# Moving the gate's four chunks and its split inside an output block, one chunk of the next layer's modulation, and one convolution tap, in a two-layer hybrid decoder kernel

## What is computed

```
mod = silu(c) @ w_ada + b_ada;  shift, scale, gate = split(mod, 3)
h   = rmsnorm(x, norm_pre) * (1 + scale) + shift
z   = h @ w_in                      # 2048 x 14336: gb, gcin, u, g_c, q, k, v, g_r
y_conv = gb * causal_conv3(gcin * u) * silu(g_c)
y_ret  = groupnorm(retention(rope(q), rope(k), v)) * silu(g_r)
o   = concat(y_conv, y_ret) @ w_out # 4096 x 2048
x   = x + gate * rmsnorm(o, norm_post)
```

## Time and profile before

| | us |
|---|---|
| median of three runs | 1730.23 |
| the profiled execution, whole | 1728.81 |
| its span, first to last instruction | 1727.0 |
| TensorE busy with matmuls | 1685.4 (98%) |
| VectorE busy | 1161.1 (67%) |
| ScalarE busy | 719.5 (42%) |

### The profile page before, as it was taken

One profiled execution on the slowest core, in us unless ns is written; L12 is line 12 of the kernel. 1 busy time (PEld: TensorE's weight loads), 2 busy tenths in 40 slices (PEclk: granted clock), 3 DMA queues, 4 the chain that ended last, 5 costly groups with the idle time before them and its releaser, 6 DMA issues. The chain is left out here.

```text
span 1727.0 us, 18943 instructions
## 1 busy us (share of the span) xinstructions
PE 1685.4 (98%) x7707; PEld 1376.3 (80%) x7707; DVE 1161.1 (67%) x1296; ACT 719.5 (42%) x802; POOL 51.0 (3%) x94
## 2 busy tenths in 40 slices
PE   6999999999999999999999999999999999999997
PEld 3567878888888888778878888888888888888886
DVE  2788767788578868777776456556555654567776
ACT  3344444434444444343455444444434444444332
POOL 4000000000000000000000000000000000000000
PEclk9999999999999999999999999999999999999999
DMA  9998655787788769877775666567556756668774
GB/s 341 383 383 316 211 180 191 271 293 263 253 289 312 270 217 323 321 274 284 282 248 164 197 203 196 189 196 219 193 178 202 216 187 189 209 242 303 290 286 179
DMA packets 233655, 429.25 MB, mean 249 GB/s; under 512 B 8664, under 2 KB 50024, under 8 KB 232800
## 3 DMA queue, kind: packets, MB, share of 16 engines
q1 hardware_dynamic: 225888, 408.97, 68.5%
q10 hardware_dynamic: 7680, 19.07, 4.0%
HBM read 417.57 MB, written 2.10 MB: 243 GB/s over the span
## 5 line engine op out<-in xcount | busy, mean ns | idle before, releaser
L809 DVE TENSOR_TENSOR w_lo<-stage,w_hi 128x1024 fp32r<-128x1024 f32 x574 | 692.9, 1223 | 467.2 <-ACT w_hi L588 464.5
L588 ACT CAST w_hi<-stage 128x1024 fp32r<-128x1024 f32 x574 | 595.7, 1051 | 945.6 <-PE Z L1275 576.2
L1273 PE MATMUL Z<-w_hi,H 128*128 128x512 f32 x1784 | 702.6, 394 | 11.0 <-DVE w_lo L809 6.4
L1275 PE MATMUL Z<-w_hi,H 128*128 128x512 f32 x1784 | 695.6, 390 | 0.0
L1274 PE MATMUL Z<-w_lo,H 128*128 128x512 f32 x1784 | 695.1, 390 | 0.0
L1273 PEld LDWEIGHTS Z<-w_hi,H 128*128 128x128 f32 x1784 | 335.3, 188 | 88.9 <-issue 8.0
L1275 PEld LDWEIGHTS Z<-w_hi,H 128*128 128x128 f32 x1784 | 335.3, 188 | 70.7
L1274 PEld LDWEIGHTS Z<-w_lo,H 128*128 128x128 f32 x1784 | 335.5, 188 | 67.9
L830 DVE SCALAR_TENSOR_TENSOR acc<-stage,c_silu,acc 128x512 f32<-128x512 f32 x240 | 180.2, 751 | 6.8
L1273 PE MATMUL Z<-w_hi,YR 128*128 128x512 f32 x256 | 100.2, 391 | 2.8 <-DVE w_lo L809 2.8
L1273 PE MATMUL Z<-w_hi,YC 128*128 128x512 f32 x256 | 99.7, 389 | 0.0
(11 more groups left out here) (160 smaller groups left out, 735.0 us busy)
## 6 DMA issues: line engine op xcount, KB each, us to landing
stage<-in_w_in SPq DMA_DIRECT2D x186, 1024.0 KB, 5.2
stage<-in_w_ada SPq DMA_DIRECT2D x64, 1024.0 KB, 7.4
stage<-in_w_out SPq DMA_DIRECT2D x64, 1024.0 KB, 7.4
stage<-in_w_in SPq DMA_DIRECT2D x74, 512.0 KB, 5.6
front_stage<-in_w_ada SPq DMA_DIRECT2D x32, 1024.0 KB, 11.2
behind<-R ACTq DMA_DIRECT2D x14, 448.0 KB, 3.5
taps<-in_conv_w ACTq DMA_DIRECT2D x18, 256.0 KB, 6.5
xt<-in_x SPq DMA_DIRECT2D x2, 1024.0 KB, 6.7
```

The source lines that it names most:

```text
L588: N.copy(w_bufs(n, h)[0], stage[:, slot_of(n), 2 * h:2 * h + 2, :]).then_inc(s_hi, 1)
L809: V.tensor_tensor(lo, stage[:, slot_of(n), 2 * h:2 * h + 2, :], hi.bitcast(F32), ALU.subtract)\
L1273: T.matmul(z[:, i, :], hh, wh, start=ch.first and a == 0, stop=False)
L1275: ins = T.matmul(z[:, i, :], hl, wh, start=False, stop=stop)
```

## The change

- The gate's chunks move from places 0, 2, 4, 5 of an output block to places 0, 2, 3, 4; in the very first output block (layer 0, block 0) they stand at 1, 2, 3, 4.
- `gate_parts` moves on VectorE from behind place 6 to behind place 5. TensorE's two matmuls stay at place 6 and `gate_row` stays at place 7.
- The first chunk of the first modulation sum of layer 1 moves from step 10 to step 11 of turn 1.
- The first tap of the first turn moves from step 9 to step 11.

The load order follows from `load_table`. In seven of the eight output blocks it becomes g0 w0 w1 g1 w2 g2 w3 g3 w4 w5 w6 w7, and in the first one w0 g0 w1 g1 w2 g2 w3 g3 w4 w5 w6 w7.

```diff
@@ FIRST
-                 tr=17, yrhi=19, yrlo=20, gcopy=99, cu=8, back=9, tap=(9, 14, 15), sg=9, gate=10,
+                 tr=17, yrhi=19, yrlo=20, gcopy=99, cu=8, back=9, tap=(11, 14, 15), sg=9, gate=10,
@@ ADA_CHUNKS
-    (1, (10, 12, 15, 16)), (1, (20, 23, 26, 27)), (2, (3, 4, 7, 8)), (2, (12, 15, 16, 18)),
+    (1, (11, 12, 15, 16)), (1, (20, 23, 26, 27)), (2, (3, 4, 7, 8)), (2, (12, 15, 16, 18)),
...
-GATE_CHUNKS, GATE_SUM, GATE_AT = (0, 2, 4, 5), 6, 7
+GATE_PARTS, GATE_SUM, GATE_AT = 5, 6, 7
+
+def gate_chunks(l, j):
+    return (0, 2, 3, 4) if l + j else (1, 2, 3, 4)
@@ load_table
-        if c.out and c.g in GATE_CHUNKS:
-            table.append(("gate", NB * c.l + c.j, GATE_CHUNKS.index(c.g)))
+        if c.out and c.g in gate_chunks(c.l, c.j):
+            table.append(("gate", NB * c.l + c.j, gate_chunks(c.l, c.j).index(c.g)))
@@ VectorE
-                if ch.out and ch.g in GATE_CHUNKS:
-                    kc = GATE_CHUNKS.index(ch.g)
+                if ch.out and ch.g in gate_chunks(ch.l, ch.j):
+                    kc = gate_chunks(ch.l, ch.j).index(ch.g)
                     ada_chunk(("gate", NB * ch.l + ch.j, kc), kc, ada_seen)
                     ada_seen += 1
...
-                if ch.out and ch.g == GATE_SUM:
+                if ch.out and ch.g == GATE_PARTS:
                     gate_parts(ch.l, ch.j)
```

## The result

The changed kernel takes 1737.27 us, the median of six runs (1735.58 to 1739.19), against 1730.08 us (1729.31 to 1731.41). The ratio is 1.0042 with a 95% interval of 1.0029 to 1.0055: slower by 7.2 us, where +4.7 was forecast.

The account below looks back on a forecast made before the run. TensorE, busy 1685.4 of 1727.0 us, was taken as the bound, so only its waits mattered. Terms 8.4 + 0.6 + 1.5 - 2.5 - 3.3 = +4.7 us gave a median of 1734.9 us, 8-in-10 range 1729 to 1740.

Parts of the forecast that it names:

- The tap: First turn's first tap, moved to step 11: the 2.51 us wait at 244.1 us goes, a gain of 2.5 us.
- The modulation chunk: Turn 1 of layer 1's first modulation sum: low parts are over 5 us early there, so priced at 0.
- The gate's split: Last block of each layer: waits of 1.88 and 1.43 us ahead of the gate's matmuls go, a gain of 3.3 us.
- The six later blocks: Blocks 1 to 3 of each layer: w4 comes late and TensorE stalls 1.4 us in each, a loss of 8.4 us.
- The deciding step: Blocks 1 to 3 of each layer: g1's slot goes to g3, so w4 lands 2.66 us later, slack 1.40 becoming -1.26 us.
- Layer 1's first block: Its w4 takes g3's place, landing after 8.9 us beside ScalarE's rows, slightly late: a loss of 0.6 us.
- The very first block: Layer 0, block 0: w3, held up by ScalarE's rows, stalls TensorE 3.5 us; present stalls go; a loss of 1.5 us.
- The signs in the profile: One w4 wait of 1.3 to 1.5 us per later block, none at gate's matmuls or 244 us, 3.5 to 4 at first-block w3.
- The faster rival: Six later blocks: w4 lands within 6.1 us of its issue, no stall, 1722 to 1725 us; chance 0.14.

Follow-up runs that it names:

- the fastest kernel: The changed kernel with w4 loaded ahead of g3 and the gate's rows fetched in quarters, those of blocks 1 to 3 one block ahead: 1719.83 us, ratio 0.9934.

## Why the prediction was right, and where it was not

**The tap** was priced at 2.5 us; 2.33 in the profile, 3.3 by the run of the tap alone, whose interval holds 2.5.

**The modulation chunk**, priced at 0, is 0.

**The gate's split**, priced at 3.3 us, brought 2.6 alone. What I said of its cause was incomplete: the new load order removes the same two waits without it, in part by making TensorE late.

**The six later blocks.** The deciding step was right: the slot of g1 goes to g3, w4 queues behind it, lands about 2.6 us later (0.41 + 7.3 - 5.1), and its slack of 1.40 us becomes a wait. Five of the six waits are 1.08 to 1.37 us. A listed wait begins at the end of the matmul before, 0.16 us behind the next start that would have been due (0.39 - 0.23), so the five starts came 1.24 to 1.53 us late, against 1.4 priced; exchanging the two loads removes them all. The term was mis-sized, 12.0 against 8.4, for three reasons.
First, the claim that the second of the pair took 7.4 to 7.5 us "in all six blocks" was wrong for block 1 of layer 0. Line 547, issued at 771.6 us in the kernel before, took this:

```profile
DMA to landing us min/median/max: 8.7/8.7/8.7
```

The changed kernel's w4 took 8.9 us in its place and waited 2.74 us, not 1.4. The other kernels show 8.5 to 8.9 us there too, so it belongs to that stretch. The DMA queues of the changed kernel from 772 to 779.7 us, while this load is under way, hold a line that they don't hold beside w4 in the next block (819.3 to 826.7 us), which took 7.3 us:

```profile
q8 instruction: 1, 0.02, 0.9%
```

This is one packet of 16 KB of instructions. 0.9% of 16 engines over 7.7 us is 1.1 us on one engine, near to the 1.3 to 1.5 us by which the load is late. In all fourteen profiles such a packet runs beside this load. In those of the kernel before and the changed one none runs beside the same loads of the other five blocks. No run moved it, so this cause isn't tested. A part of the error is the prediction's own besides: it priced all six blocks with a slack of 1.40 us, though it had read 0.96 us in this one.
Second, behind that wait the clock fell. The drop and the restart made another 1.4 us (4.26 lost, 2.90 of them up to w4's start). The prediction had no term for the clock and read it as full "in all slices of the page". A slice of the page is 43 us long and its digit 9 means 90% or more, so it hides the drop that a window from 92 to 96 us shows in the profile before (a mean granted clock of 0.57).
Third, each of the five other waits cost 0.15 us more than the late start, because the first matmuls behind it start further apart (0.33 us, then 0.23).

**Layer 1's first block** was priced at 0.6 and cost 2.0. I had put w3 in the place of g2, landing after 9.8 us. It stood behind g2 and took 11.4 us beside the rows; g3 and w4 then queued behind it, and w4 took 9.8 us where I had 8.9. The step that went wrong is the single price of 8.9 us, taken from a queue with less ahead of it.

**The very first block** was priced at +1.5 and cost +1.7, with a wait of 3.38 us at w3 (3.5 predicted) and w3's landing after 11.0 us (11 predicted). But part of the sum was luck. No wait came at w5, where 0.6 us was priced, and a drop of the clock, which was not, filled its place.

**The signs in the profile** came as listed: a wait at w4 in each of six blocks, g3 in 5.0 and w4 in 7.3 us, nothing at 244 us and at the gate's matmuls. The output blocks waited 14.1 us against 13 predicted. The faster rival, in which the pair doesn't queue, is ruled out: w4 never landed within 6.1 us behind g3. The rule of the Trainium skill (page "DMA: Bandwidth & Descriptors", section "Queues, rings and completion order"), that completion isn't first in, first out, did not help here: in the output blocks every load of SyncE's queue landed behind the one issued before it, in all fourteen profiles. The rule is borne out elsewhere. In the start-up of the kernel before, the load that line 540 issues at 42.46 us landed after 11.0 us, and the one that line 560 issues at 42.87 us after 10.0 us, so ahead of it; every profile has this pair.

**A reading that was wrong.** The prediction puts the 9.2 us in six waits "behind the start-up". Three of them (1.51, 0.64 and 1.74 us) stand at 30, 58 and 64 us. No term of the sum used them.

## What to carry to other kernels

Where few slots are shared by two streams of loads, ask for each slot that comes free which load takes it, and put the one that the bound engine needs next ahead of the one that only fills a sum. Look for the load that has the least slack in each period, not for the engine with the most work. A burst on another queue can't be judged by its size alone (cut into 2 x 256 KB, it used the DMA engines for longer per byte), and moving it moves the wait; give it a place where the loads beside it have slack to spare.

## What the runs showed of the hardware

After the start-up, the granted clock fell to half for 3.4 us at the end of each of the five waits of 2.7 us or more, or right behind it (2.74, 3.38, 3.52, 3.70 and 4.37 us; with the last for 6.8 us, of which 2 us lie in the wait). Behind waits of 2.1 to 2.6 us it fell in some executions and not in others, and never behind the waits at w4 of 1.1 to 1.8 us.

What a drop costs depends on what bounds the stretch: 1.6 us behind the wait at 244 us, about 1.4 us with the restart in block 1 of layer 0, and nothing near 92 us, where TensorE waits for others anyway. The kernel before spreads over up to 5.5 us (21 runs on one chip), the fastest kernel, with no wait of over 0.7 us in its output blocks, over 0.9 us (5 runs). The drops may be a part of this; no run tested it.

The gate's rows as 2 x 256 KB on ScalarE's queue held up a load of SyncE's queue by 3 us for 0.5 MB: 109 GB/s at a busy share of 0.95. As 2 x 1 MB they moved at 406 GB/s.

The second load of 1 MB of the pair w4 and g3, issued 0.4 us behind the first, took 7.3 to 7.5 us in five blocks of the kernel before and the changed one. In the sixth, where a 16 KB packet of instructions ran beside it, it took 8.5 to 8.9 us in all fourteen profiles.
